# Reordering the opening weight loads of a two-block transformer kernel and splitting one projection of its memory values

## The reference

```python
u = rms_norm(h, norm1_g) * (1 + scale1) + shift1
z = u @ w_in                      # values, keys, queries, gates of both attentions
...                               # block-sparse and stick-breaking attention, up projections
h = h + gate1 * mixed
u2 = rms_norm(h, norm2_g) * (1 + scale2) + shift2
h = h + gate2 * (square(relu(u2 @ mlp_w1)) @ mlp_w2)
```

```python
x = x + 0.5 * swiglu(rmsnorm(x, ffn1_norm), ...)     # f1
z = rmsnorm(x, mix_norm) @ w_in_2                    # mixing norm, then cq, ckv, kr, qm, ...
```

## Time and profile before

| | |
|---|---|
| median of 3 runs (lowest, highest) | 1139.22 us (1138.97, 1141.1) |
| the profiled execution, its span | 1141.08 us, 1139.4 us |
| TensorE matmul busy | 1100.3 us (97%) |
| VectorE, ScalarE, POOL busy | 746.5, 589.3, 59.4 us |
| mean granted TensorE clock | 0.988 |
| DMA | 209.11 MB, mean 184 GB/s |

### The profile page before, as it was taken

The page is one execution under the profiler, slowest core; times in us unless marked ns, Lnnn a source line. Parts: engine busy times, 40 slices in busy tenths (PEclk is TensorE's granted clock), DMA queues, the critical chain, the costliest instruction groups (busy, mean ns, idle before and its releaser), DMA issues.

```text
span 1139.4 us, 21787 instructions
## 1 busy us (share of the span) xinstructions
PE 1100.3 (97%) x8478; PEld 1056.2 (93%) x8478; DVE 746.5 (66%) x1258; ACT 589.3 (52%) x1041; POOL 59.4 (5%) x86
## 2 busy tenths in 40 slices
PE   5899799999999999999999999999999999999999
PEld 2699698889989999999999998989989999999998
DVE  3658688867578764446666545567776877666643
ACT  2375375655465554445444434678645356444432
POOL 3013111000100000000000000000000002000000
PEclk9899799999999999999999999999999999999999
DMA  9768875245545555555555554444433455555553
GB/s 360 272 219 302 310 240 205 75 130 170 182 166 180 182 180 184 184 185 184 179 182 181 184 184 147 152 158 154 149 111 121 158 169 167 184 184 185 186 185 111
DMA packets 58515, 209.11 MB, mean 184 GB/s; under 512 B 7055, under 2 KB 8591, under 8 KB 57912
## 3 DMA queue, kind: packets, MB, share of 16 engines
q1 hardware_dynamic: 51320, 180.00, 47.4%
q0 software_dynamic: 7104, 27.81, 6.8%
HBM read 204.62 MB, written 3.16 MB: 182 GB/s over the span
## 4 chain that ended last, share of the span: by engine, by line
PE 84%; DVE 6%; DMA 5%; ACT 4%; issue 1%; SPq 0%; DVEq 0%; ACTq 0%
PE bank L633 83%; DMA ada_ring<-in_ada 3%; DMA wide<-in_ada 2%; DVE ada_acc L1757 2%; DVE ring_rounded L1687 1%; ACT rounded_rounded L1271 1%; PE bank L894 1%; ACT wide L1453 1%; SPq L585 0%; ACT wide_rounded L1320 0%; DVE wide_rounded L1731 0%; ACT wide L1379 0%; DVE kcat L1847 0%; DVE x L2017 0%; DVE u_lo_rounded L1833 0%
## 5 line engine op out<-in xcount | busy, mean ns | idle before, releaser
L1687 DVE TENSOR_TENSOR ring_rounded<-ring,rounded_rounded 128x1024 fp32r<-128x1024 f32 x326 | 398.5, 1226 | 259.0 <-ACT rounded_rounded L1271 252.6
L633 PE MATMUL bank<-u_rounded,rounded_rounded 128*128 128x256 f32 x1528 | 440.0, 288 | 6.6 <-DVE ring_rounded L1687 3.0
L633 PE MATMUL bank<-u_rounded,ring_rounded 128*128 128x256 f32 x1528 | 433.6, 284 | 0.0
L633 PE MATMUL bank<-u_lo_rounded,rounded_rounded 128*128 128x256 f32 x1528 | 431.8, 285 | 0.5 <-DVE u_lo_rounded L2069 0.5
L1271 ACT ACTIVATE rounded_rounded<-ring 128x1024 fp32r<-128x1024 f32 x326 | 342.2, 1053 | 170.1 <-PE bank L633 148.3
L633 PEld LDWEIGHTS bank<-u_rounded,rounded_rounded 128*128 128x128 f32 x1528 | 295.5, 193 | 12.0 <-issue 6.2
L633 PEld LDWEIGHTS bank<-u_lo_rounded,rounded_rounded 128*128 128x128 f32 x1528 | 293.3, 193 | 3.3 <-DVE u_lo_rounded L1733 1.5
L633 PEld LDWEIGHTS bank<-u_rounded,ring_rounded 128*128 128x128 f32 x1528 | 295.5, 193 | 0.0
L633 PE MATMUL bank<-shared_rounded,rounded_rounded 128*128 128x256 f32 x1024 | 258.6, 284 | 0.0
L633 PE MATMUL bank<-wide_rounded,rounded_rounded 128*128 128x256 f32 x832 | 222.5, 283 | 1.2 <-DVE shared_rounded L1988 1.2
L633 PE MATMUL bank<-wide_rounded,ring_rounded 128*128 128x256 f32 x736 | 208.3, 283 | 0.0
(11 more groups left out here) (290 smaller groups left out, 1057.1 us busy)
## 6 DMA issues: line engine op xcount, KB each, us to landing
ring<-in_stream SPq DMA_DIRECT2D x328, 512.0 KB, 3.3
ada_ring<-in_ada POOLq DMA_DIRECT2D x35, 512.0 KB, 5.5
wide<-in_ada SPq DMA_DIRECT2D x6, 512.0 KB, 17.6
shared<-in_ada POOLq DMA_DIRECT2D x4, 512.0 KB, 15.7
mem_parts_kept<-wide_rounded POOLq DMA_DIRECT2D x2, 1024.0 KB, 5.6
shared_rounded<-mem_parts_kept POOLq DMA_DIRECT2D x2, 1024.0 KB, 6.0
x<-in_x_t SPq DMA_DIRECT2D x2, 512.0 KB, 6.2
wide<-in_mem_t SPq DMA_DIRECT2D x2, 512.0 KB, 5.8
```

The source lines that it names most:

```text
L633: return nc.tensor.matmul(out, lhs, rhs, start=start, stop=stop, skip_group_check=True)
L1687: v.tensor_tensor(R(w), w, R(slot_round(q)), ALU.subtract).then_inc(slot_split, 1)
```

## The change

Five things are edited.

1. **Start.** The scale's chunks stand first in both queues: POOL's order is scale 0, 1, 3 to 7, then shift 5 and 7; SP's is scale 2, then shift 0 to 4 and 6. Slot 0 of the weight stream is loaded after all of them. x_ss comes first on TensorE, slot 0 is rounded after the norm's factor is made, and VectorE splits it in the middle of the eight scaled chunks of x.
2. **Memory forward.** mem's squares are made by ScalarE right after u, added by VectorE (not POOL), summed on TensorE after vsb1; the norm of mem is made before the bias is copied. POOL stores the two parts right after it sends the bias out, and before it loads it back.
3. **adaLN steps.** 14 steps stand before the heads, 10 inside them, and 8 (all of ada5) in the first eight of the MLP's blocks w1. `ada_part(3)` moves to head 3, 4 to after mb0, 5 to after w1_9; the steps for the rotary angles start at w1_10.
4. **Memory values.** Only heads 0 and 1 (256 columns, two slots) stand beside the norm of ROW_1. Heads 2 and 3 are projected around x3_ss; the memory parts are loaded again for them during f1.
5. POOL's loads of the spatial gating weights follow the last ada chunk.

```diff
-ADA_BY_POOL_QUEUE = ((0, 0), (1, 0), (1, 1), (0, 2), (0, 3), (1, 5), (0, 4), (0, 5), (0, 7))
-ADA_BY_SP_QUEUE = ((0, 1), (1, 2), (1, 3), (1, 4), (1, 6), (1, 7), (0, 6))
+ADA_LATE = 40
+ADA_BY_POOL_QUEUE = ((1, 0), (1, 1), (1, 3), (1, 4), (1, 5), (1, 6), (1, 7), (0, 5), (0, 7))
+ADA_BY_SP_QUEUE = ((1, 2), (0, 0), (0, 1), (0, 2), (0, 3), (0, 4), (0, 6))
...
@@ SP
-            for part_and_chunk in ADA_BY_SP_QUEUE[:4]:
+            for part_and_chunk in ADA_BY_SP_QUEUE:
                 load_ada_early(*part_and_chunk)
             sp.dma_start(mats[:, MAT["ident"], :], mats_d[:, MAT["ident"], :]).then_inc(ident_loaded, 16)
-            load(0, 0)
-            for part_and_chunk in ADA_BY_SP_QUEUE[4:]:
-                load_ada_early(*part_and_chunk)
-            for r in range(1, 4):
+            for r in range(4):
                 load(r, r)
...
@@ TensorE
-            pe.wait_ge(c_spread_ready, 1)
-            shift_block(0)
             pe.wait_ge(ones_ready, 2)
             sum_row("x_ss", ROW_X, merged)
-            for k in range(1, 5):
+            pe.wait_ge(c_spread_ready, 1)
+            for k in range(SHIFT_BEFORE_SCALE):
                 shift_block(k)
...
             project_tokens(["vsb0", "vsb1"], KD, u_parts, 512)
+            ps = claim("mem_ss")
+            pe.wait_ge(mem_summed, 3)
+            done(mm(ps[:, 0:T], mat("ones"), mem_squares[:, 0, :], True, True), "mem_ss")
...
-            project_tokens(["mem_v0", "mem_v1"], KD, mem_parts, 512, lambda: sum_gathered("x1_ss", ROW_1))
+            project_tokens(["mem_v0", "mem_v1"], KD, mem_parts, 256, lambda: sum_gathered("x1_ss", ROW_1))
...
-            sum_gathered("x3_ss", ROW_3)
+            pe.wait_ge(loaded["mem_again"], 32)
+            project_tokens(["mem_w0", "mem_w1"], KD, (mem_hi_again, mem_lo_again), 256, lambda: sum_gathered("x3_ss", ROW_3))
...
@@ POOL
             pool.dma_start(bias_rows, bias_line).then_inc(bias_stored, 16)
+            pool.wait_ge(u_rounded, (ROW_MEM + 1) * KD)
+            pool.dma_start(mem_parts_kept[0], R(mem_n)).then_inc(mem_stored, 16)
+            pool.wait_ge(u_ready, (ROW_MEM + 1) * KD)
+            pool.dma_start(mem_parts_kept[1], R(mem_n_lo)).then_inc(mem_stored, 16)
             pool.wait_ge(bias_stored, 16)
...
@@ ScalarE
-            ahead("x_ss", 1)
-            row_inv("x_ss", 1)
+            row_inv("x_ss", 0)
             ahead("x_ss", HALVES)
...
+            act.wait_ge(loaded["mem"], 16)
+            row_square(mem_squares, mem_n, lambda i: act.wait_ge(loaded["mem_end"], 16) if i == KD // 2 else None)
             act.wait_ge(zeros_ready, 4)
...
@@ VectorE
+            ahead("vsw1")
+            dve.wait_ge(row_squares_ready, (ROW_MEM + 1) * KD)
+            for i, n in enumerate((4, 2, 1)):
+                v.tensor_tensor(mem_squares[:, 0:n, :], mem_squares[:, 0:n, :], mem_squares[:, n:2 * n, :], ALU.add).then_inc(mem_summed, 1)
+                dve.wait_ge(mem_summed, i + 1)
+            ahead("vsb1")
+            norm_row(mem_n, mem_n_lo, mem_n, gains("mem_norm_2"), ROW_MEM, None, lambda: ahead("ga"))
             output("bias")
...
-                for _ in range(2 if h < 6 else 1):
+                for _ in range(2 if h in (0, 5, 6) else 1 if h < 7 else 0):
                     ada_step()
...
             for m in range(KF):
+                if m < KD:
+                    ada_step()
+                if m == 10:
+                    ada_reduce(5)
```

More of the change, by code:

```diff
@@ L265, in proj_names @@
     out = ["x_ss"]
[L266 to L270, removed]
+    out += ["vsw0", "vsw1", "vsb0", "vsb1", "mem_ss", "ga", "bias", "kc", "vc", "ks", "kw"]
+    out += [f"qa{b}" for b in range(4)] + [f"kb{b}" for b in range(4)] + [f"qb{b}" for b in range(4)]
+    out += ["ada2", "cmp_hid_k", "cmp_hid_v", "ma0", "cmp_turn_k", "cmp_turn_v"]
+    out += ["ga_turn", "ma1", "cmp_out_k", "cmp_out_v", "ma2", "ma3", "ada3", "ma4", "ma5", "ma6", "ma7"]
+    out += ["mb0", "ada4"] + [f"mb{b}" for b in range(1, 8)]
     for m in range(KD):
@@ L273, in proj_names @@
     out += [f"mix{m}" for m in range(KD)]
-    out += [f"w1_{m}" for m in range(KF)] + [f"w2_{m}" for m in range(KD)]
+    out += [f"w1_{m}" for m in range(10)] + ["ada5"] + [f"w1_{m}" for m in range(10, KF)]
+    out += [f"w2_{m}" for m in range(KD)]
     def swiglu(p):
@@ L784, in _ @@
             done(ada_columns(claim("ada1"), 1, 0), "ada1")
-            for k in range(5, KD):
+            for k in range(SHIFT_BEFORE_SCALE, KD):
                 shift_block(k)
@@ L952, in _ @@
                 if i == 0:
-                    ada_part(5)
+                    ada_part(4)
                 if i:
@@ L978, in _ @@
                 project(f"w1_{m}", KD, u_parts)
+                if m == 9:
+                    ada_part(5)
             for m in range(KD):
@@ L1252, in _ @@
                                pattern=[[0, 8], [1, P]], channel_multiplier=-1).then_inc(sg_w_ready, 1)
-            for row, last in ((ROW_2, "w2_"), (ROW_3, "f1d"), (ROW_4, "mix2_")):
+            gather_squares(ROW_2, "w2_")
+            full(pool, f"w2_{KD - 1}")
+            pool.dma_start(R(mem_hi_again), mem_parts_kept[0]).then_inc(loaded["mem_again"], 16)
+            pool.dma_start(R(mem_lo_again), mem_parts_kept[1]).then_inc(loaded["mem_again"], 16)
+            for row, last in ((ROW_3, "f1d"), (ROW_4, "mix2_")):
                 gather_squares(row, last)
@@ L1508, in _ @@
             for t in range(TT):
-                copy(mem_v[:, t, :], f"mem_v{t}", bank(f"mem_v{t}")[:, :])
+                copy(mem_v[:, t, 0:256], f"mem_v{t}")
             nc.scalar.preload_act_table_set("silu_and_others")
@@ L1559, in _ @@
             round_row(ROW_3, u, u_lo)
+            for t in range(TT):
+                copy(mem_v[:, t, 256:512], f"mem_w{t}")
             def latent_block(i, name, gain, k):
@@ L1857, in _ @@
                 ada_step()
-            norm_row(mem_n, mem_n_lo, mem_n, gains("mem_norm_2"), ROW_MEM, None, lambda: ahead("qb0"))
-            for b in range(3):
+            for b in range(4):
                 ahead(f"qb{b}")
@@ L1862, in _ @@
             ada_reduce(2)
-            for _ in range(3):
-                ada_step()
-            ada_reduce(3)
-            for _ in range(2):
-                ada_step()
+            ada_step()
             before = mat("before")
@@ L2061, in _ @@
                     rest_of_hidden(m - 1, m - 1)
-                next(steps, None)
+                if m > 9:
+                    next(steps, None)
             rest_of_hidden(KF - 1, KF - 1)
+            dve.wait_ge(mod_ready, 4)
             def add_and_split(last, gate, gain, row, reach_later=False):
```

80 lines of the change are left out of this document (29 added, 51 removed).

## The result

The changed kernel takes 1128.68 us (median of 5 runs, 1127.38 to 1132.6) against 1139.22 before: ratio 0.9911, 95% interval 0.9891 to 0.9931. It is faster by 10.5 us. The forecast was 1119, its range 1115 to 1127: the direction was right, half of the gain did not come, and the time lies 1.7 us outside the range. The profiled execution took 1130.33 us, with a span of 1128.6.

A forecast was written before the change was run, and what follows sets the result against it. TensorE works 97% of the span, so only its opening, waits and low-clock stretches were open to gain. Terms -6.4 + 1.4 - 0.9 + 1.5 - 8.9 - 5.6 - 0.8 - 0.5 - 0.1 = -20.3 gave 1119 us, range 1115 to 1127.

The forecast's parts named there:

- edit 2's +1.4: First projection to qa0: ScalarE's wait for mem and later splits of slots 4, 5 and 10 cost 1.4 us, bounds 0 and +5.
- rival (e): ScalarE, in order, waits for mem and everything behind it waits too, making the kernel slower than before; chance 3%.
- Each us beyond 48 costs one: Price within the slower-than-before rival: each us ScalarE waits for mem past 48 costs one; passing 1139 needs landing after about 68.
- mem landing beyond 48: Sign that the forecast is wrong: mem's load lands after 48 us, where 45 to 47 was expected.
- the idleness above 1 us between 37 and 85: Sign for the forecast: TensorE has no idleness above 1 us between 37 and 85 us.
- Start, -6.4: Kernel's opening: scale chunks first bring the first projection to 36.8 from 43.26 us, 6.4 us gained, bounds 0 and -8.
- The waits and the clock behind them, -8.9 and -5.6: Ahead of the heads: TensorE's waits of 3.0 and 5.9 us go, and the clock behind both stays full, saving 5.6.
- POOL's additions, -0.9: Without POOL's additions (85.97 to 92.35 us) slowing VectorE, TensorE's wait of 0.9 us right behind them goes.
- Late ada loads, +1.5: POOL's mem stores delay the bias and ada loads; kb2 starts at 93.9 instead of 92.4 us: +1.5, bounds 0 and +6.
- Head 2, -0.8, head 7, -0.5: One ada step instead of two at head 2 removes 0.8 us; none left at head 7 starts its chain 0.5 earlier.
- Memory's values, -4.2 and +4.1: Splitting memory's values saves 4.2 us at ROW_1 and costs 4.1 at ROW_3, net -0.1, bounds -2 and +3.
- w1, 0: In the MLP's w1, eight ada steps replacing rotary steps cost TensorE nothing; without VectorE's lead, +2 us.

The follow-up runs named there:

- experiment 5: The changed kernel with its start undone (old ada_w chunk order, shift block 0 ahead of x_ss, first split where it was): 1127.45 us, ratio 0.9887.
- experiment 6: The kernel before with only the new start put in (early ada_w chunk order, x_ss ahead of shift block 0, later first split): 1133.72 us, ratio 0.9937.
- Experiment 7: Changed kernel with ScalarE's vsw copies ahead of its wait for mem, plus ada_part(3) back ahead of the heads with 16 ada steps before it: 1131.95 us.
- experiment 3: The changed kernel with vsb1 put in a PSUM bank of the attention scores, ScalarE's order unaltered: 1123.39 us, ratio 0.9847.
- experiment 8: Experiment 7's kernel with the bias loaded back ahead of the two stores of mem on POOL's queue: 1131.53 us, ratio 0.9927.
- experiment 9: Changed kernel with ScalarE's vsw copies ahead of its wait for mem, plus memory's values projected whole at the first norm: 1119.61 us, ratio 0.9828.
- experiment 10: Changed kernel with ScalarE's vsw copies ahead of its wait for mem, plus x3_ss after two of mem_w's eight chunks, not four: 1119.15 us.
- experiment 12: Experiment 9's kernel with x1_ss taken after two of eight chunks of memory's values instead of four: 1118.81 us, ratio 0.9814.
- experiment 2: The changed kernel with only slot 4's rounding moved ahead of ScalarE's wait for mem: 1126.16 us, ratio 0.9879.

## Why the prediction was wrong

**The step that failed is edit 2's +1.4.** The prediction saw the right cause, as rival (e): ScalarE stands in order for mem, mem lands at 45 to 47 (it landed at 45.3 and 46.6), ScalarE stands until 48 (47.9). It then named what stands behind the wait as "the rounding of slot 4 and its split (1.06 + 1.2: 50.3), which TensorE wants at 50.0", and that split too came when it said: the split ended at 50.13. What it left out is the third thing behind the same wait, the copies that free vsw0's bank, which vsb1 claims at 44.6 and not at 50. A wait of 0.2 became one of 4.7, and behind it came the half clock, 2.4 more. Its price for rival (e), "Each us beyond 48 costs one", was wrong for the same reason: each us costs one by which the copies of vsw0 end after 44.6, and they ended at 49.19. Its sign of being wrong, "mem landing beyond 48", did not appear; the idleness above 1 us between 37 and 85 that it excluded did.

**The missed wait is one that edits 1 and 2 make together.** The start moved TensorE 6.3 us forward and mem's landing by less: its load was issued 7 us sooner, at 34.1, but took 11.6 us to land (the page's median) where it took 5.8. With the old start there is no wait ahead of vsb (experiment 5), and without mem's squares there the start keeps its gain (experiment 6). The prediction did price edit 2 with the new start's times, but only for the one thing that it saw behind the wait. With the old start the claim on the bank comes near 50.4 (42.83 + 7.6 in experiment 5) and meets only 0.2 us of wait.

Point by point, the rest:

- *Start, -6.4*: right, -6.3. TensorE's last shift block ends at 34.1, forecast 34; the full clock held until 37.4. The half clock behind it, at 37.5 to 40.8, cost next to nothing: vsw, which follows VectorE's splits, took 7.6 us against 7.45.
- *The waits and the clock behind them, -8.9 and -5.6*: right in size, with POOL's term: qa0 to ma0 is 16.3 us shorter against 15.7. Experiment 7 shows what did it for the 5.9 and its clock, the two ada steps fewer, and that the rival "VectorE's list" is wrong there; for the 3.0 the cause is argued only.
- *POOL's additions, -0.9*: the wait is gone in the changed kernel, but it is back at 0.3 to 0.7 in the profiles of experiments 3, 7, 8, 9, 10 and 12, which have none of these additions. So how much of it was theirs is not shown.
- *Late ada loads, +1.5*: not there. The loads were even later than forecast (the stores took 7.8 us and not 5.6, the bias 14.1, the first load was issued at 90.9, not 87), and VectorE waited for them, 7.6 us in all; TensorE has no wait from 79.8 to ma0. The mechanism is real but had cover. (In edit 3, three in flight at 8 us give one each 2.7 us, not 2.9; nothing hung on it.)
- *Head 2, -0.8, head 7, -0.5*: the wait of 0.8 at the split output went. The first profile shows +0.3 for ma0 to mb0, with a wait of 1.1 behind the rounding of a late weight slot and the clock behind that in it; in the second profile of the same kernel this stage came out about 2 us shorter. At head 7 nothing was won: the wait for the turned copy is 1.8, as before.
- *Memory's values, -4.2 and +4.1*: right to 0.1. The half clock at ROW_3, which the +4.1 took as gone, came back in the first profile (1.2 us).
- *w1, 0*: right. TensorE's stretch there grew by the columns alone, 1.8.

Of the rivals none took place; (e) named ScalarE's wait for mem, with a chance of 3% for going past 1139, and no case stood for it at a smaller size. That is why 1128.7 lay outside the range: edit 2 cost 8.4 where its bound was +5, and the bound had no term for the clock behind a wait.

## What to carry over

When an in-order engine gets a new wait, list everything behind it on that engine up to the latest time the wait can end, and for each entry who is waiting, with the buffers that it frees as well as the data that it makes; a PSUM bank handed back is easy to overlook, as no data flows through it. A stage that starts sooner meets transfers that come hardly sooner: redo every claim behind the latest wait, the banks too, with the new starting time. Where a norm behind a sum is the path, the sum's place in the filler work sets the end, and moving it costs one argument (1.6 us at the second norm here; at the first, with the whole values, 1.5 of 2.7 came).

## What the runs showed of the hardware that was not expected

- The clock behind a wait is partly chance. Two profiles of the same program had 16.7 and 9.9 us at 0.50, with equal medians (1128.68 and 1128.74). At the second norm the changed kernel's wait of 0.52 had a half clock behind it, and experiment 2's, also 0.5, had none, as its window there shows:

```profile
688.00:702.00 14.00, 13.48 (x95) 11.88 (x94) 10.62 (x19) 9.62 (x19) 0.00 (x0) 1.00 0.42 139
```

  By these two profiles a single one tells the clock's cost only to some 3 us: half of 16.7 - 9.9 (an estimate).
- Reordering POOL's queue gave no time back (1131.95 to 1131.53 us): with the bias ahead, it took 8.7 instead of 14.8 us, and the stores 13.2 instead of 7.5, the ada chunks 9.4 instead of 6.3.
